# One f32r pass over stacked value halves for the sample-state product of an SSD layer

## What is computed

```
def step(s, inp):
    qc, kc, vc, lac = inp
    cum = jnp.cumsum(lac, axis=1)
    ...
    tail = jnp.exp(cum[:, -1:, :] - cum)
    s_new = jnp.exp(cum[:, -1, :])[..., None, None] * s + jnp.einsum('bjhd,bjh,bjhe->bhde', kc, tail, vc)
    return s_new, intra + cross
```

## Time and profile before

| | |
|---|---|
| time, median of 3 runs | 2132.25 us (2130.79 to 2140.04) |
| profiled execution | 2139.35 us, span 2137.6 us |
| granted clock of TensorE, mean (1 is full speed) | 0.976 |
| TensorE busy | 2031.3 us, 95% of the span |
| TensorE weight loads busy | 1854.1 us, 87% |
| VectorE busy | 1295.4 us, 61% |
| ScalarE busy | 890.2 us, 42% |
| GpSimd busy | 384.3 us, 18% |

### The profile page before, as it was taken

One profiled execution on the slowest core, in us unless ns is written; L12 is line 12 of the kernel. 1 busy time (PEld: TensorE's weight loads), 2 busy tenths in 40 slices (PEclk: granted clock), 3 DMA queues, 4 the chain that ended last, 5 costly groups with the idle time before them and its releaser, 6 DMA issues. The chain is left out here.

```text
span 2137.6 us, 40735 instructions
## 1 busy us (share of the span) xinstructions
PE 2031.3 (95%) x14070; PEld 1854.1 (87%) x14070; DVE 1295.4 (61%) x1929; ACT 890.2 (42%) x1947; POOL 384.3 (18%) x554
## 2 busy tenths in 40 slices
PE   6999999999899997999889999999999999977998
PEld 6999999999777776788789999999999999956887
DVE  7755899776456567333234767675767676685422
ACT  6221212233344455223244555554555555465331
POOL 0200000000122221000000434343434333350000
PEclk9999999999999998999999999999999999998999
DMA  4433333332688798244522333333333333285331
GB/s 134 132 103 103 93 101 104 111 112 78 200 289 267 253 313 294 84 128 138 152 73 56 82 94 93 84 85 85 83 93 96 94 82 86 65 257 150 116 126 40
DMA packets 386859, 274.10 MB, mean 128 GB/s; under 512 B 117609, under 2 KB 342601, under 8 KB 386601
## 3 DMA queue, kind: packets, MB, share of 16 engines
q1 hardware_dynamic: 338806, 242.77, 38.6%
q10 hardware_dynamic: 47850, 28.76, 4.5%
HBM read 184.59 MB, written 86.88 MB: 127 GB/s over the span
## 5 line engine op out<-in xcount | busy, mean ns | idle before, releaser
L1586 PE MATMUL p3acc_ps<-xn2hi,p3whi 128*128 128x272 f32 x1536 | 461.6, 301 | 6.3 <-ACT p3mid L1789 3.7
L1586 PE MATMUL p3acc_ps<-xn2lo,p3whi 128*128 128x272 f32 x1536 | 445.9, 290 | 0.0
L1586 PE MATMUL p3acc_ps<-xn2hi,p3wlo 128*128 128x272 f32 x1536 | 445.5, 290 | 0.0
L269 PE MATMUL p1ps<-x1hi,w1hi 128*128 128x272 f32 x1288 | 373.0, 290 | 4.7 <-issue 3.1
L269 PE MATMUL p1ps<-x1hi,w1lo 128*128 128x272 f32 x1288 | 372.8, 289 | 0.0
L269 PE MATMUL p1ps<-x1lo,w1hi 128*128 128x272 f32 x1288 | 371.8, 289 | 0.0
L1586 PEld LDWEIGHTS p3acc_ps<-xn2hi,p3whi 128*128 128x128 f32 x1536 | 292.6, 190 | 7.7 <-issue 7.3
L1586 PEld LDWEIGHTS p3acc_ps<-xn2lo,p3whi 128*128 128x128 f32 x1536 | 292.8, 191 | 0.2
L1586 PEld LDWEIGHTS p3acc_ps<-xn2hi,p3wlo 128*128 128x128 f32 x1536 | 292.2, 190 | 0.0
L269 PEld LDWEIGHTS p1ps<-x1hi,w1hi 128*128 128x128 f32 x1288 | 243.3, 189 | 5.0 <-issue 5.0
L269 PEld LDWEIGHTS p1ps<-x1hi,w1lo 128*128 128x128 f32 x1288 | 243.7, 189 | 0.0
(11 more groups left out here) (330 smaller groups left out, 4289.9 us busy)
## 6 DMA issues: line engine op xcount, KB each, us to landing
w1raw<-in_ret_w_in SPq DMA_DIRECT2D x48, 512.0 KB, 5.0
p3raw<-in_ssm_w_in SPq DMA_DIRECT2D x48, 512.0 KB, 4.5
ret_vg<-y1out SPq DMA_DIRECT2D x32, 512.0 KB, 3.2
r_vg<-ret_vg SPq DMA_DIRECT2D x32, 512.0 KB, 5.3
r_sin<-in_state_ret SPq DMA_DIRECT2D x32, 512.0 KB, 6.5
out_ret_sample<-r_sout ACTq DMA_DIRECT2D x32, 512.0 KB, 6.6
s_cr<-sums SPq DMA_DIRECT2D x64, 256.0 KB, 3.4
ret_qk<-y1out SPq DMA_DIRECT2D x16, 512.0 KB, 3.7
```

The source lines that it names most:

```text
L269: last = nc.tensor.matmul(bank[:, 2 * at + i, 0:HB], w[s][:, idx, k, :], x[:, idx, k, i * HB:(i + 1) * HB], start=(k == 0 and j == 0), sto ...
L1586: last = nc.tensor.matmul(pr_ps[:, n % 2, 0:TB], wt[:, j % 2, k, :], x[:, k, b * TB:(b + 1) * TB], start=(k == 0 and i == 0), stop=(k == K ...
```

## The change

The state product becomes one f32r pass over 96 rows. A half `u` of the sequences (0 to 3, or 4 to 7) has 32 positions. Its keys stand on three quarters of 32 rows each as high, high and low half (`bst[:, u]`), its values so that the quarters hold the pairs high x high, high x low and low x high (`vst[:, u]`). `own` masks all 96 rows at once, and the eight-row sets of one sequence are summed by one product. Around this:

- ScalarE: `by_tokens(g, NCH)` makes four copies of 32x128 more (L1848 of the changed kernel), which round the keys to f32r. `sample_values_high` (L1903) is new: four copies of 32x256, behind `square(g, 0)` and ahead of the sample decay; it waits for GpSimd's `vts`. `own(g, 0)` moves from behind `by_tokens` to behind the evacuation of unit 2 and waits for the low half of the keys.
- VectorE: `sample_keys_low` (L2272), two subtractions of 32x128, and `sample_values_low` (L2278), two of 32x256 behind the weights' low half, are new.
- TensorE: `sample(g, 0)` moves from ahead of unit 3 to behind the scores of chunk 2, ahead of unit 4, and waits for the low half of the values (`v_low`) instead of `vts`.
- GpSimd no longer writes the zeros, SP loads another mask of 128x8, and an unused tile that keeps room shrinks.

The diff, cut to its core:

```diff
+        "seqcol_four": (i[:, None] % (NS // 2) // DS == np.arange(DB)[None, :] % (DB // 2)).astype(f),
...
-        bm = sb(ctx, "s_bm", [P, 2, P], F32)
+        bst, bm = sb(ctx, "s_bst", [P, 2, P], F32R), sb(ctx, "s_bm", [P, 2, P], F32R)
...
+        vst = sb(ctx, "s_vst", [P, 2, W], F32R)
...
+        QUARTER, STACK = NS // 2, 3 * NS // 2
+        quarters = [slice(i * QUARTER, (i + 1) * QUARTER) for i in range(4)]
...
                     held(pe, q["b_own"], 8 * g + c + 1 + B, passed)
-                    nc.tensor.matmul(sb_ps[:, 0:W], bm[:, s, :], vts[:, :, :].rearrange("p h n -> p (h n)"),
+                    nc.tensor.matmul(sb_ps[:, 0:W], bm[0:STACK, s, :], vst[0:STACK, c // 4, :],
                                      start=True, stop=True).then_inc(q["sb_mm"], 1)
...
-                        if c == 1:
-                            held(pe, q["vt"], prep(g, NCH) + 1 + B, passed)
-                            sample(g, 0, par, more)
                         if more:
                             unit(g + 1, 3 * c)
...
+                        if c == 1:
+                            held(pe, q["v_low"], g + 1 + B, passed)
+                            sample(g, 0, par, more)
                         if more:
                             unit(g + 1, 3 * c + 1)
...
-                    nc.scalar.activation(b_dst[0:r, :], t_ps[0:r, 0:P], ACT.Copy).then_inc(q["tok"], 1)
+                    last = nc.scalar.activation(b_dst[0:r, :], t_ps[0:r, 0:P], ACT.Copy)
+                    if c == NCH:
+                        for u in range(2):
+                            for rows in quarters[0:2]:
+                                last = nc.scalar.activation(bst[rows, u, :], t_ps[quarters[u], 0:P], ACT.Copy)
+                    last.then_inc(q["tok"], 1)
...
-                    nc.scalar.activation(bm[0:NS, c % 2, :], btoks[:, :], ACT.Copy,
-                                         scale=seqcol[:, c:c + 1]).then_inc(q["b_own"], 1)
+                    nc.scalar.activation(bm[0:STACK, c % 2, :], bst[0:STACK, c // 4, :], ACT.Copy,
+                                         scale=seqcol[0:STACK, c:c + 1]).then_inc(q["b_own"], 1)
+
+                def sample_values_high(g):
+                    held(act, q["vt"], prep(g, NCH) + 1 + B, passed)
+                    for u in range(2):
+                        for rows in (quarters[u], quarters[2]):
+                            last = nc.scalar.activation(vst[rows, u, :], vts[quarters[u], :, :].rearrange("p h n -> p (h n)"),
+                                                        ACT.Copy)
+                    last.then_inc(q["v_high"], 1)
...
-                            act.wait_ge(q["tok"], prep(g, NCH) + 1 + B)
-                            own(g, 0)
                         if more:
                             project(g + 1, 3 * c + 2, 1 - par, beyond)
+                        if c == 0:
+                            held(act, q["b_low"], g + 1 + B, passed)
+                            own(g, 0)
                         square(g, c)
                         if c == 0:
+                            sample_values_high(g)
                             decay(g, NCH, decs)
                             exp_sums(g, NCH, ers, crws)
...
-                nc.gpsimd.memset(bm[NS:P, :, :], 0.0).then_inc(zeroed, 1)
-                nc.gpsimd.memset(vts[NS:P, :, :], 0.0).then_inc(zeroed, 1)
-                pool.wait_ge(zeroed, 4)
...
+                def sample_keys_low(g):
+                    held(dve, q["tok"], prep(g, NCH) + 1 + B, passed)
+                    held(dve, q["b_own"], 8 * g + B, passed)
+                    for u, rows in enumerate(quarters[0:2]):
+                        last = nc.vector.tensor_tensor(bst[quarters[2], u, :], btoks[rows, :], bst[rows, u, :], ALU.subtract)
+                    last.then_inc(q["b_low"], 1)
+
+                def sample_values_low(g):
+                    held(dve, q["v_high"], g + 1 + B, passed)
+                    for u, rows in enumerate(quarters[0:2]):
+                        last = nc.vector.tensor_tensor(vst[quarters[1 - u], u, :], vts[rows, :, :].rearrange("p h n -> p (h n)"),
+                                                       vst[rows, u, :], ALU.subtract)
+                    last.then_inc(q["v_low"], 1)
...
                         if c == 0:
+                            sample_keys_low(g)
                             held(dve, q["ins"], 16 * (g + 1) + B, passed)
...
                             project(g + 1, 3 * c + 2, 1 - par, beyond)
+                        if c == 0:
+                            sample_values_low(g)
```

More of the change, by code:

```diff
@@ L1309, in phase_ssd @@
         least_s = sb(ctx, "s_least_s", [NS, NS], F32)
-        seqcol = sb(ctx, "s_seqcol", [NS, DB], F32)
+        seqcol = sb(ctx, "s_seqcol", [P, DB], F32)
         cr = sb(ctx, "s_cr", [P, SL, SHG, P], F32)
@@ L1330, in phase_ssd @@
         btoks, xtoks = sb(ctx, "s_btoks", [NS, P], F32), sb(ctx, "s_xtoks", [NS, W], F32)
-        sb(ctx, "room_tok", [P, 6 * W], F32)
-        bm = sb(ctx, "s_bm", [P, 2, P], F32)
+        sb(ctx, "room_tok", [P, 3 * W], F32)
+        bst, bm = sb(ctx, "s_bst", [P, 2, P], F32R), sb(ctx, "s_bm", [P, 2, P], F32R)
         vt, vts = sb(ctx, "s_vt", [P, 2, SHG, SHD], F32), sb(ctx, "s_vts", [P, SHG, SHD], F32)
+        vst = sb(ctx, "s_vst", [P, 2, W], F32R)
         dec, decs = sb(ctx, "s_dec", [P, 2, SHG, P], F32), sb(ctx, "s_decs", [NS, SHG, NS], F32)
@@ L1359, in phase_ssd @@
                  "g_out0", "g_out1", "g_out2", "ss_out0", "ss_out1", "ss_out2", "st_mm", "st_dec", "st_add", "sb_mm", "s_mid",
-                 "sb_add", "b_own",
+                 "sb_add", "b_own", "b_low", "v_high", "v_low",
                  "raw0", "raw1", "w_hi", "w_lo", "p_mm", "p_ev", "pre", "first", "tap", "taps", "tails", "tanh", "fin")
@@ L1537, in _ @@
                                  allow_slow_non_contiguous=True).then_inc(consts, 16)
-                for dst, name in ((least_s, "least_s"), (seqcol, "seqcol")):
+                for dst, name in ((least_s, "least_s"), (seqcol, "seqcol_four")):
                     sp.dma_start(dst[:], A[name]).then_inc(consts, 16)
@@ L1757, in _ @@
                 dma_wait(pe, consts, 4)
-                pe.wait_ge(zeroed, 4)
+                pe.wait_ge(zeroed, 2)
                 group(0, 0, first=True)
@@ L2025, in _ @@
                         sample_exponents()
-                act.wait_ge(zeroed, 4)
+                act.wait_ge(zeroed, 2)
                 steps_over(act)
@@ L2380, in _ @@
                 dma_wait(dve, consts, 4)
-                dve.wait_ge(zeroed, 4)
+                dve.wait_ge(zeroed, 2)
                 group(0, 0)
```

## The result

The changed kernel takes 2141.03 us (median of 20 runs, 2131.18 to 2150.02) against 2131.51 us before (20 runs). The ratio is **1.0052, with a 95% interval of 1.0039 to 1.0065**: some 10 us slower, where 4 us faster was forecast. The profiled execution of after took 2149.27 us with a span of 2147.5, 9.9 us above the span of before; the mean granted clock is 0.968 instead of 0.976. Both profiled executions lie some 8 us above the medians of their kernels.

The account below looks back on a forecast made before the run. TensorE, busy for nearly the whole span, was taken as the bound. Saved passes -17.2, new waits +11.2 and group 7 +2 sum to -4.0 us: 2128 us against the median 2132.25, range 2117 to 2142.

Parts of the forecast that it names:

- The saving: TensorE's state products, groups 0 to 6: one f32r pass saves 0.31 us each over 56 products, -17.2 us.
- The rival by which 96 rows cost more: State product on TensorE: a partial-row pass costs 0.32 us more per visit, 17.9 us over 56, 2146 us; chance 0.06.
- The place of the wait and its chain: TensorE before each group's first sample product waits for values' low half, via ScalarE and VectorE: 1.6 us each, +11.2.
- the start that was due: TensorE reaches sequence 0's new place behind chunk 2's score products 0.88 us earlier than before, at 1283.3.
- VectorE's key subtractions: Two subtractions ahead of the sample mask, taken to fit in VectorE's 3.83 us of idle time before 1280.17.
- the rival of a short wait: Value copies on ScalarE overlap like full-height ones, so the wait is 0.8 us: 2120.6 us; chance 0.14.
- The two value subtractions: VectorE behind the weights' low half: two 32x256 operations at 0.45 us each, 0.9 us in all.
- The bounds: Limits of TensorE's new wait: 0.8 us with copies at 0.30, near 1.9 with VectorE's chunk masks slowed beside GpSimd.
- The rival that got 0.09: TensorE returns at 1.2 GHz after each new wait: seven times 2.1 us waiting plus 1.7 us lost, 2143.6 us; chance 0.09.
- the deciding point: Length of a TensorE wait after which its clock falls: about 2 us, 0.4 beyond the central wait.
- Group 7: Last group, a chain without cover: of 2.0 + 0.9 us of delay, +2 us carried to the end (0.5 to 3.5).

Follow-up runs that it names:

- the run of the pass alone: The kernel before with the state product's operands written as f32r, one pass on 128 rows in the old order, nothing else added: 2115.72 us, ratio 0.992.
- the last run: The change with value copies ahead of unit 2's evacuation, value subtractions behind the sample mask, sample tokens announced before the key copies: 2113.41 us, ratio 0.9918.

## Why the prediction was wrong

**The saving** (17.2 us; 56 x 0.31 is 17.4) was right: 0.31 us per product in the run of the pass alone, and 2.49 us per group. The rival by which 96 rows cost more fell with the 0.21 us of the built pass. The Trainium skill's rule that changing the tiling mode drains TensorE ("TensorEngine Tiling (Array Packing)", section "Key Properties") would have mattered if the pass counted as another mode; the trace prints its tile as 96*128, and the next product follows after 0.21 us, so nothing drained. The prediction had taken the tile as full.

**The place of the wait and its chain** were right. Its size was the first step that failed: 1.6 us a group were taken, with 1.9 as the upper end, and +11.2 in all. From the start that was due to the one that came, the seven waits of after are 2.1 to 2.6 us, 17.2 in all, as much as the passes save. The second step that failed is the clock, which the sum has at nothing. Group 1 of after shows the terms. ScalarE's and VectorE's timelines, and GpSimd's beside them:

```profile
1279.14 0.40 ACT L1793 ACTIVATE p3mid<-p3acc_ps 128x272 f32<-128x272 f32 x1 [1.28 <-PE p3acc_ps L1590]
1279.85 0.40 ACT L1896 ACTIVATE s_bm<-s_bst,s_seqcol 96x128 fp32r<-96x128 f32 x1 [0.31 <-DVE s_bst L2272]
1280.15 0.40 ACT L1879 ACTIVATE s_sq<-s_gn 128x256 f32<-128x256 f32 x1
1280.46 1.68 ACT L1903 ACTIVATE s_vst<-s_vts 32x256 fp32r<-32x256 f32 x4
1282.17 0.31 ACT L1855 ACTIVATE s_decs<-s_decs 64x128 f32<-64x128 f32 x1
```

```profile
1278.19 1.48 DVE L2272 TENSOR_TENSOR s_bst<-s_btoks,s_bst 32x128 fp32r<-32x128 f32 x2 [2.06 <-ACT s_bst L1848]
...
1282.99 0.41 DVE L2245 TENSOR_TENSOR s_decs<-s_decs,s_ps 64x256 f32<-64x256 f32 x1 [2.62 <-ACT s_decs L1857]
1283.33 1.21 DVE L2182 TENSOR_TENSOR p3wlo<-p3raw,p3whi 128x1024 fp32r<-128x1024 f32 x1
1284.57 1.16 DVE L2278 TENSOR_TENSOR s_vst<-s_vts,s_vst 32x256 fp32r<-32x256 f32 x2
```

```profile
1278.22 0.72 POOL L2081 TENSOR_TENSOR s_vts<-s_xtoks,dtail 64x256 f32<-64x256 f32 x1 [1.01 <-ACT s_bst L1848]
1278.91 0.60 POOL L2145 TENSOR_TENSOR s_smid<-s_sin,etot_s 128x256 f32<-128x256 f32 x1
...
1284.69 0.77 POOL L2081 TENSOR_TENSOR s_vt<-s_xtok,dtail 128x256 f32<-128x256 f32 x1 [3.60 <-ACT s_btok L1844]
```

- The evacuation at 1279.14 to the square at 1280.15 is 1.01 us; 0.60 was forecast. The mask (L1896) waited 0.31 us for VectorE's key subtractions, which the prediction had called hidden: two operations of 32x128 took 1.48 us while GpSimd's decayed values (1278.22) and its next product (1278.91) ran; the first took 0.28, the second 1.18, up to 0.15 us behind the end of that next product. In the last run, where GpSimd has done that product earlier, they take 0.58.
- The four copies take 1280.46 to 1282.17, 1.71; 1.68 was forecast. These copies on changing partitions did not overlap, and the rival of a short wait fell with that.
- The two value subtractions took 1.16 instead of 0.9, again beside a GpSimd product (1284.69).
- They end at 1285.73, and TensorE's first product starts at 1286.39. I had put 0.3 us there (1.6 less 1.3); it is 0.66.

From the start that was due, 1283.55 + 0.22, to 1286.39 this is 2.62 us, against 1.6 + 0.41 + 0.26 + 0.36 = 2.63; the trace's 2.39 counts from the end of the last product. The bounds named GpSimd only for the chunk masks, and the way from one engine's end to another's start was not read from the trace of before at all.

**The clock.** The rival that got 0.09 had the mechanism right, and its time (2143.6 forecast, 2141.0 measured) came close in part by luck: it had seven waits of 2.1 us and seven falls of 1.7, 26.6 us, and what came were 17.2 us of waits and five falls of some 1.5. Two steps made its chance so small: the wait was undersized by 1 us, and the deciding point was read as a sharp one, at about 2 us, from one wait with and one without a fall. The trace of before itself shows no such point. Two waits of TensorE, each of 2.55 us, one in the retention stage and one in the SSD stage, and the stretches behind them:

```profile
810.03 0.49 PE L939 MATMUL r_misc<-r_sq,r_ones 128*128 128x128 f32 x2 [2.55 <-ACT r_kt L1046]
1469.28 0.30 PE L1594 MATMUL s_ps<-s_ident,p3zb 128*128 128x128 f32 x1 [2.55 <-issue]
```

```profile
810.00:814.00 4.00, 3.97 (x33) 3.89 (x34) 3.18 (x4) 1.98 (x4) 0.09 (x1) 1.00 0.83 259
1470.50:1473.90 3.40, 3.40 (x17) 3.40 (x17) 0.95 (x3) 0.55 (x2) 0.42 (x1) 0.50 0.28 66
```

The first was followed by full clock, the second, at the turn of the loop in group 3, by half clock. The later runs say the same of the waits for the changed chain: behind waits of up to 1.0 us none in 14 groups (two runs), behind 1.2 to 1.5 us two in seven, behind 1.9 to 2.4 us five in seven, behind 2.9 to 3.2 us seven in seven. Waits of equal length go either way. A fall cost 1.4 to 1.5 us between groups with nearly the same wait, a little under the 1.7 that was used.

**The sum in its own terms.** The trace of after has -17.4 for the passes, +17.2 for the waits, some +7.5 for five falls of the clock and +3.0 for group 7, which makes +10.3, in place of -17.2 + 11.2 + 2. Groups 0 to 7 together lost 12.4 us; the other 2 us are not settled. By these terms the waits take back the whole saving, and most of the slowdown is the clock.

**Group 7** cost 3.0 us instead of 2, within its bounds, and 1.6 of it is left in the run whose value chain starts earliest.

## What to carry to other kernels

Where one engine has no idle time, a saving on it is worth what the slowest new chain in front of it leaves over, so the added work on idle engines should be placed by where they are idle, and not behind what the busy engine waits for next: the same operations gave 1.0052 and 0.9918. A wait of TensorE is to be priced with the chance that it returns at half clock, and in these runs that chance does not begin at a sharp length. When a wait is taken away, look for the second consumer of the same delay; here it was the weights' low half.

## What was not expected of the hardware

Waits of only 1.5 us were followed by half clock in two cases of four, and behind the waits of sequence 0 a stretch of half clock was 3.4 us long in most cases and 6.8 in two, behind waits of 3.1 us. Small VectorE operations with two operands in SBUF took more than double the time beside GpSimd products: 1.48 us against 0.58 for the same two subtractions. The Trainium skill states that such operations read their second operand through an interface shared with GpSimd ("VectorE: DVE Perf Modes", section "Two Vector instructions with no wait between them"); the trace agrees with that, though no run here takes GpSimd's product away by itself.
